# A hybrid decoder layer on one core: the first 256 tokens' trunk rewritten in two halves of 128, with scaling by the root mean square after the first products

## The reference

```python
h = rmsnorm(x, norm_mix)
u_s5, x_lru, y_lru, g_a, g_b = split(h @ w_in)          # 512, 512, 512, 1024, 1024 columns
a_out = S5(u_s5)        # complex diagonal scan over time, 32 groups of 64 states, then gelu, GLU (w_glu)
b_out = RG-LRU(x_lru, y_lru)   # conv of width 4, two gates, real scan over time
merged = sigmoid(g_a) * (a_out @ w_proj_a) + sigmoid(g_b) * (b_out @ w_proj_b)
x = x + merged @ w_out
x = x + peer(rmsnorm(x, norm_ffn))
def peer(xc):           # 8 heads
    q = xc @ w_q;  s = q . sub_keys                     # 2 x 128 scores for each head
    16 best of each 128, 16 best of the 256 sums -> eidx, softmax g
    act = gelu(u_tab[eidx] . xc);  out = sum over 128 experts of g * act * v_tab[eidx]
```

## Time and profile before

| | |
|---|---|
| median of 3 runs | 3243.57 us (3235.98 to 3243.91) |
| profiled execution | 3249.83 us, span 3247.7 us |
| mean granted TensorE clock | 0.934 |
| busy share of the span | PE 84%, PE weight load 48%, DVE 77%, POOL 38%, ACT 30% |
| DMA | 1251.68 MB, mean 385 GB/s; gathers 1082.20 MB |
| first gather issued | 251.13 us |
| largest shares of the chain that ended last | gathers 40%, `values` (L1740) 13%, `dots` (L1410) 10% |

### The profile page before, as it was taken

The page is one execution under the profiler, slowest core; times in us unless marked ns, Lnnn a source line. Parts: engine busy times, 40 slices in busy tenths (PEclk is TensorE's granted clock), DMA queues, the critical chain, the costliest instruction groups (busy, mean ns, idle before and its releaser), DMA issues.

```text
span 3247.7 us, 31396 instructions
## 1 busy us (share of the span) xinstructions
PE 2714.0 (84%) x9120; PEld 1542.8 (48%) x9120; DVE 2493.6 (77%) x5858; ACT 976.4 (30%) x3001; POOL 1225.6 (38%) x1048
## 2 busy tenths in 40 slices
PE   7988988998979989888778989899888895666566
PEld 6874544565445445555334545556434442222122
DVE  6836888888679888887679888887668886666754
ACT  2113433232134332322134332322123432222223
POOL 0003344344343444344343443343344343545553
PEclk9999999999989999999989999998999997878789
DMA  4369999999999999999999999999999999999997
GB/s 136 95 212 396 403 419 420 409 396 419 418 417 385 411 420 419 381 420 419 418 418 400 418 417 403 387 416 374 417 401 418 420 395 298 421 407 421 422 422 332
DMA packets 208636, 1251.68 MB, mean 385 GB/s; under 512 B 27961, under 2 KB 36537, under 8 KB 76369
## 3 DMA queue, kind: packets, MB, share of 16 engines
q0 software_dynamic: 148608, 1082.20, 81.3%
q1 hardware_dynamic: 57344, 158.97, 13.2%
q10 hardware_dynamic: 2512, 8.52, 0.7%
HBM read 1245.05 MB, written 4.55 MB: 385 GB/s over the span
## 4 chain that ended last, share of the span: by engine, by line
DMA 41%; PE 26%; DVE 21%; issue 3%; ACT 3%; DVEq 2%; POOL 2%; ACTq 1%; POOLq 0%
DMA arena<-in_uv,arena 40%; PE psum L1740 13%; DVE arena L1410 10%; PE psum L1661 6%; DVE arena L1015 4%; DVE arena L1007 3%; ACT arena L692 2%; POOL arena L651 2%; PE psum L1784 2%; PE psum L1796 1%; DVE arena L1256 1%; PE psum L1775 1%; PE psum L1674 1%; PE psum L1694 1%; PE psum L1646 1%
## 5 line engine op out<-in xcount | busy, mean ns | idle before, releaser
L1740 PE MATMUL psum<-arena 128*128 128x512 f32 x3192 | 1606.7, 647 | 463.8 <-ACT arena L692 430.8
L651 POOL DMA_INDIRECT arena<-in_uv,arena x1032 | 1221.6, 1184 | 1994.7 <-PE psum L1740 1381.0
L1410 DVE CUSTOM_DVE_ANT_0 arena<-arena 128x1024 f32<-128x1024 f32 x1024 | 1237.2, 1224 | 529.6 <-DMA arena<-in_uv,arena 498.4
L1740 PEld LDWEIGHTS psum<-arena 128*128 128x128 f32 x3192 | 620.2, 202 | 1303.6 <-ACT arena L692 642.1
L692 ACT ACTIVATE arena<-arena 128x128 f32<-128x128 f32 (+3 forms) x2481 | 699.0, 313 | 1633.7 <-DVE arena L1410 1478.4
L1661 PE MATMUL psum<-arena 128*128 128x256 f32 (+1 forms) x2688 | 622.5, 387 | 12.0 <-DVE arena L1015 6.4
L1661 PEld LDWEIGHTS psum<-arena 128*128 128x128 f32 x2688 | 515.4, 193 | 143.5 <-issue 71.3
L1015 DVE SCALAR_TENSOR_TENSOR arena<-arena 128x1024 f32<-128x1024 f32 (+6 forms) x477 | 392.7, 830 | 66.8 <-ACT arena L692 35.9
L1007 DVE TENSOR_TENSOR arena<-arena 128x256 f32<-128x256 f32 (+10 forms) x832 | 285.0, 382 | 24.1 <-issue 1.7
L692 ACT ACTIVATE arena<-psum 128x256 f32<-128x256 f32 (+7 forms) x266 | 107.3, 414 | 554.5 <-PE psum L1661 481.4
L692 ACT ACT_TABLE_LOAD x113 | 145.0, 1283 | 3.9 <-PEq L2040 0.8
(11 more groups left out here) (97 smaller groups left out, 949.4 us busy)
## 6 DMA issues: line engine op xcount, KB each, us to landing
arena<-in_w_in SPq DMA_DIRECT2D x112, 512.0 KB
arena<-in_w_q SPq DMA_DIRECT2D x68, 512.0 KB
arena<-in_w_ab SPq DMA_DIRECT2D x40, 512.0 KB
arena<-in_w_out SPq DMA_DIRECT2D x40, 512.0 KB
arena<-in_uv,arena POOLq DMA_INDIRECT x1032
arena<-in_w_glu SPq DMA_DIRECT2D x16, 256.0 KB
arena<-in_x_tok SPq DMA_DIRECT2D x8, 512.0 KB
arena<-in_keys SPq DMA_DIRECT2D x32, 128.0 KB
```

Source lines behind the costliest of these rows:

```text
L651: pool.indirect_dma_start(uvring[:, r], None, i_["uv"], bass.IndirectOffsetOnAxis(column, 0)).then_inc(uv_in[r], 16)
L1410: V.tensor_tensor_reduce(out=u, in0=u, in1=hn[i // (SLOT // 2)], scale=1.0, scalar=0.0, op0=ALU.mult, op1=ALU.add, accum_out=dots_[:, b % ...
L1740: ins = mm(PV[:, half], dg[:, PAIR * (b % 2) + k], uvring[:, i % UV, at:at + 512], start=(i % (SLOT // 2) == 0), stop=(pe_slots(c, i + 1) ...
```

## The change

Only chunk 0's stretch up to the end of its own steps is rewritten, as one `first_chunk` on each engine; chunks 1 to 3 keep their code, with other counts.

1. **Scaling after the first products.** DVE writes `gb = hT * nmix` as the four parts of `hT` arrive; PE multiplies the four u units with those, the first ahead of the sum of squares, and `scaled_u` multiplies the products with `rstd` on the way out of PSUM (DVE, in place of an ACT copy). `hT` itself is scaled meanwhile, for the units after. SP issues the parameters of the step size first, then `hT`, the first weights, then the rest.
2. **S5 and LRU in halves.** `s5_in_half(k, jp)`, `s5_out_half`, `s5_half`, `lru_half`, `z_half` do the tokens of tile k. Tile 0 goes through S5, LRU, GLU, `mix`, `out` first. Tile 1's S5 stands between `out`, transposes, queries and scores of tile 0 on PE, and around the first list on DVE.
3. **Four heads alone.** Heads 0 to 3 of tile 0 are ranked alone (ALONE = 4), heads 4 to 7 for both tiles, heads 0 to 3 of tile 1 last, two in a round. w_glu is loaded a second time for tile 1, and eight w_q slots in place of four: SLOTS0 = 92.
4. **Steps.** OWN0 = 57 in place of 48, so 71 steps are left for chunk 1's trunk in place of 80. `on_dve` starts at step 57 in chunk 0, not 48. The first steps (t = 96 to 114) run under the lists of heads 1 to 3, `mix` and `out` of tile 1.

The last two pieces of the diff are the heads alone on ACT, and on DVE what follows the norm of tile 0.

```diff
-OWN0 = 48
+OWN0 = 57
+ALONE = 4
-U_MIX0, U_OUT0, U_MIX1, U_Q0, U_OUT1, U_Q1, UNITS0 = 40, 48, (56, 57, 58, 59, 62, 63, 66, 67), (60, 64), 68, 76, 92
+U_GLU1, U_MIX1, U_OUT1, U_Q1, UNITS0 = 64, 68, 76, 84, 100
 SLOTS0 = UNITS0 - 8
+IN_AT, OUT_AT, GATES_AT = (0, 1, 3, 5, 6, 8, 9, 10), (5, 5, 6, 7, 9, 10, 11, 12), 8
-    first, whole, last = (32, 82, 108) if c else (48, 90, 111)
+    first, whole, last = (32, 82, 108) if c else (57, 94, 112)
...
-            weights0 = trunk + mix + out + mix[0:4] + query[0:2] + mix[4:6] + query[2:4] + mix[6:8] + out \
-                + query[4:16] + query[0:4]
+            weights0 = trunk + mix + out + query[0:2 * ALONE] + trunk[28:32] + mix + out \
+                + query[2 * ALONE:] + query[0:2 * ALONE]
...
+            for k in range(KT):
+                if k % 2 == 0:
+                    dve.wait_ge(x0_in[k // 2], 16)
+                ts(gb[:, k, 0:C], hT[:, k, 0:C], nmix[:, k:k + 1]).then_inc(hx_ok, 1)
+            def scaled_u(q):
+                dve.wait_ge(unit, U_U + q + 1)
+                tt(halves(uS[:, q, 0:C]), parities(PB[q % 2][:, 0:C]), parities(rstd[:, 0:C]), ALU.mult).then_inc(ue_ok, 1)
...
+            def s5_in_half(k, jp):
+                q, done = jp // 2, SJ // 2 * k + jp
+                need(pe, bu_read, done)
+                pe.wait_ge(ue_ok, q + 1)
+                for j in (2 * jp, 2 * jp + 1):
+                    o = 32 * (j % 4)
+                    for part in range(2):
+                        for r in range(2):
+                            at, src = 2 * SEG * part + SEG * k, 2 * SEG * r + SEG * k
+                            ins = mm(SB[j % 2][:, at:at + SEG], wT[o:o + 32, QT * (2 * r + part) + q],
+                                     uS[o:o + 32, q, src:src + SEG], start=(r == 0), stop=(r == 1))
+                ins.then_inc(bu_ok, 1)
...
+                for h in range(ALONE):
+                    for s in range(2):
+                        query(U_Q0 + 2 * h + s, s, qT0[:, s])
+                    if h == 2:
+                        soft(0, P, 1, alone)
+                    scores(h, flat(sS0[:, h]), PV[:, h % 2, 0:2 * NKEY])
...
+                pieces(scans[1], PIECES + 1)
+                for _ in single(0):
+                    pass
+                dve.sem_inc(idx_ok, 1)
+                pieces(scans[1], 3 * PIECES)
+                for piece, _ in enumerate(single(1)):
+                    if piece == 0:
+                        a_half(E_GLU1, LATE)
+                    upto(at0_q(1) + piece + 1)
+                    if piece == 1:
+                        mix(0, U_MIX1, LATE, MIXB[0])
+                    if piece >= 1:
+                        mix(piece, U_MIX1 + piece, LATE, MIXB[piece % 2])
```

More of the change, by code:

```diff
@@ L1 @@
+from collections import namedtuple
 from contextlib import ExitStack
@@ L376, in build @@
         hn = [R.take(D) for _ in range(2)]
-        acc = [R.take(D) for _ in range(2)]
+        acc = [R.take(D)]
+        acc1_at = R.at
+        acc.append(R.take(D))
         dg = R.take(2 * PAIR, P)
@@ L1496, in scale, with a_half, single @@
                     stt(hn_at[t], x2_at[t], ss[:, t:t + 1], weights, ALU.mult, ALU.mult).then_inc(hn_ok, 1)
-                early, late = slice(0, P), slice(P, C)
+                def a_half(e, cols):
+                    for q in range(QT):
+                        dve.wait_ge(evac, e + q + 1)
+                        stt(rT[:, q, cols], rT[:, q, cols], 1.0, yS[:, q, cols], ALU.add, ALU.mult).then_inc(a_ok, 1)
+                def single(h):
+                    dve.wait_ge(s_ev, h + 1)
+                    yield from topk(h, P, 1, lambda t: gn[:, h], lambda t: idxn[:, h], sS0[:, h], alone)
@@ L1565, in chunk @@
                         next(gates)
-                    elif not first:
+                    else:
                         conv(c, convs, last)
@@ L1816, in first_lists @@
-                for m in range(3):
-                    mix1(m)
+                    if k == 2:
+                        s5_in_half(1, 1)
+                    elif k == 4:
+                        s5_out_half(1, 0)
+                        s5_in_half(1, 2)
+                    elif k == 6:
+                        s5_out_half(1, 1)
+                        s5_in_half(1, 3)
+                    out(0, 40 + k, k, [(0, P, 0)])
+                s5_out_half(1, 2)
+                s5_in_half(1, 4)
                 pe.wait_ge(hn_ok, 1)
@@ new lines, in first_chunk @@
+                s5_out_half(1, 5)
+                s5_in_half(1, 7)
+                s5_out_half(1, 6)
+                s5_out_half(1, 7)
+                pe.wait_ge(z_ok, 2 * QT)
+                for q in range(QT):
+                    pe.wait_ge(evac, E_GLU1 + q - 1)
+                    apply(U_GLU1 + q, 48 + 2 * ALONE + q, yS, QT, LATE)
+                for m in range(KT):
+                    upto(at1_mix(m))
+                    if m == 0:
+                        pe.wait_ge(lru_ok, 2 * QT)
+                        pe.wait_ge(a_ok, 2 * QT)
+                        pe.wait_ge(bu_read, SJ)
+                    if m >= 2:
+                        pe.wait_ge(mix_ok, KT + m - 1)
+                    mix(0, U_MIX1 - 8 + m, LATE, MIXB[m % 2], rT)
@@ L1876, in chunk @@
                 upto = paced(batches, c)
[L1877 to L1878 removed]
+                steps = s5_steps(c, n)
                 due = [next(steps)]
```

721 lines of the change are left out of this document (456 added, 265 removed).

## The result

The changed kernel takes **3256.57 us** (median of 5 runs, 3252.45 to 3260.43), beside 3243.57 us of the kernel before: ratio 1.0046, 95% interval 1.0030 to 1.0061. It is slower by 0.46%. The forecast, 3239.7 and "no change", was wrong; the range, up to 3258, held the time. (The ratio is that of the record, over all the runs; the two medians alone give 1.0040, 13.0 us.) A second series of the same kernel gave 1.0032 (1.0020 to 1.0044), so its loss is 10 to 15 us. The profiled execution took 3252.45 us, its span 3250.6.

A forecast was written before the change was run, and what follows sets the result against it. Compute was taken to bound the first 251 us, DMA traffic the 3000 us after. Terms: 24.8 - 18 - 1 - 2 = 3.8 us gained, 3246.0 profiled, 3239.7 as median, "no change"; eight in ten 3223 to 3258.

The forecast's parts named there:

- The start: Launch to first gather, where compute sets the pace: first gather at 226.3 us, 24.8 earlier; bounds 219 and 236.
- What the full stretch must carry: From the first gather on: 7.4 MB more left to move at 412 GB/s, 18 us back; total 1254.6 MB.
- First steps, 1 us back: Chunk 0's first steps: ring traffic until about 254 us, gather 8 at 254; 1 us lost, bounds 0 and 8.
- Steps, 2 us back: Nine steps moved from chunk 1's trunk to chunk 0, PE closer to traffic there: 2 us lost, bounds -3 and 10.
- Rival B: First steps, t = 96 to 117, go at the engines' pace: 13 us lost, start slips 5, 3258; chance 0.19.
- A: Start: halves cost half, PE's clock rises early, first gather at 219; 13 gained, 3230, or 3224; chance 0.32.
- C: Start: weights or DVE's table chain hold PE, first gather at 238; 8 lost, 3251; chance 0.09.
- the first gather is early and the traffic behind it is not full: Sign, around and after the first gather, that would show the forecast wrong; expected DMA share 1.0 from 228 us.

The follow-up runs named there:

- e11_more_mb: The kernel before with 3.15 MB of loads that nobody reads added in chunks 1 to 3: ratio 1.0024.
- e1_own57: The kernel before with 57 own steps in chunk 0 in place of 48 and the DVE rows moved with them: ratio 1.0016.
- the mended kernel: The changed kernel with first-steps waits reordered and the very first step ahead of tile 1's GLU and `mix`: 1.0000 with 57 own steps, 0.9993 with 48.
- e10_early52: The mended kernel with 52 own steps in chunk 0: ratio 0.9986, 3240.41 us beside 3244.73 of the kernel before; repeated, 0.9985.
- e5_own48: The changed kernel with 48 own steps in chunk 0 in place of 57, spread over the same 57 units: ratio 1.0023.
- e7_all: The changed kernel with 48 spread own steps, tile 1's columns copied earlier, DVE's first `dots` before its GLU products, and PE's `mix` and step order edited: 1.0010.
- e9_early48: e7_all (48 spread own steps) plus the very first step taken ahead of the second tile's GLU and `mix`: ratio 0.9993.

## Why the prediction was wrong

*The start:* right. 28.5 us against 24.8. The first unit at 11.74 (11.5 forecast), the granted clock 1.00 between 10 and 60 us (2.4 GHz), units' end 60.08 (60.4), `mix` 155.61 (156.9). `s5_in_half` took 1.60 us busy and 1.53 to the next row, near the whole `s5_in`, as chosen (1.9 with its turnround, so 0.3 too much each). The page "TensorE: Matmul & The Clock Gate" of the Trainium skill, section on LDWEIGHTS, had said that a load takes the time of its columns: the trace agrees, 1.46 us for the 16 loads of 32 rows and 128 columns here against 1.52, and 0.73 for the 16 loads of 128 rows and 32 columns in `s5_out_half`. (That is half for a quarter of the columns.) The latter's products fell from 1.53 to 0.89 (1.1 forecast). The first list ended at 222.18, where the exponentials had been allowed until 225.5 and 0.6 more.

*What the full stretch must carry:* right. 33.7 MB by 222 us (33.4 forecast by 226), 1254.65 MB in all (1254.6), 17.3 us for the bytes where 18 stood, and the price per MB by `e11_more_mb`, within its interval.

*First steps, 1 us back:* this is the step that failed; some 10 us were lost from 250 to 520 us. The ninth gather was forecast at 254 and went at 256.14, and the ring's traffic, said to last "until about 254", ended by 250, since the first gather had come earlier too: the overlap that the sum counted on had a hole of 6 us in it, and the share of 250 to 260 fell to 0.69. The early first step alone gave back about 5.5 us. The prediction had even written down the cause, "steps, POOL and PE's `values` all stand behind the GLU", and then priced it at 1. The waits at the second tile's columns, 4.88 and 5.14 us on PE and 14.43 on POOL, had no term at all; moving one copy there gave 5 to 10 by the ratios, 1 to 3 at gather 256.

*Steps, 2 us back:* too small as well; chunk 1's trunk lost about 7 us. `e1_own57` has 5 us for the moved steps alone; in the mended kernel it is 2 (1.0000 against 0.9993, intervals overlapping), or 4.5 to 5 against 52 steps (0.9986 and 0.9985). The working compared PE's sum with the traffic's over the whole trunk, and both fitted; the loss is local, where a chain without steps outlasts the ring (share 0.61 and 0.64 at 990 to 1010 us).

*Rival B* gave 3258, nearly the measured time, and a dip at 250 to 260 us, which came. That its number fits is luck: its mechanism, engines too slow for a step of 6.4 us "below 400 GB/s until 370", is not what happened: from 300 to 350 us the share is 1.02 at 416 GB/s, and changes of order and of the number of steps, which shorten no instruction, took the losses away. Its working also sets 382 GB/s against a 420 that the earlier trace rows doesn't have; against the 412 there its 13 us would be 10. Only its slip of the first steps was real. *A* said 219 for the first gather, as far from the 222.67 measured as the forecast's 226.3; its input halves at half price didn't come, and it failed behind the first gather where the forecast did. *C* didn't come.

The sum, then: 28.5 gained, 17.3 for bytes, 18 lost behind the first gather where 3 stood, about 7 behind at 1200 us. The prediction had named this sign against itself: "the first gather is early and the traffic behind it is not full". The ratios' 10 to 15 us are more than these 7; their intervals reach down to 6.5. Chunks 2 and 3 show no further loss that stands out from single executions: from gather 512 to 640 the changed kernel falls 3.3 us further behind, but there the kernel before took 369.8 us, the least of all the profiles, and the others 370.4 to 374.0. Open too is the rest of the lead: with both losses mended, some 11 us should be left, and `e10_early52` shows 4.5 to 4.9 in its ratios and 5 to 9 at gather 256.

## What to carry to other kernels

Here a transfer that started earlier gained only as many bytes as the buffers held until their first consumer ran: follow the ring's ninth place, not its first, and put the first consumer ahead of any wait that it doesn't need. When work is moved under a trunk or out of it, don't compare sums over the whole stretch; find the longest chain without a step and ask whether the ring outlasts it. Where nearly every byte counts, price added loads at bytes over the measured rate.

## What the runs showed beyond that

- The ring of eight gathers, issued from 222.67 to 231.57 us, was dry by 250: with the weights loaded beside it, the share was 1.01 from 227 to 250 us and 0.46 in the next 2 us. A stretch of 11.5 to 11.8 us without gathers, near 990 us, emptied it too: with 71 steps to 96 units the unused time there was 8.1 us in the changed kernel, with 80 it was 5.2 in the kernel before and 2.0 to 2.6 in `e5_own48`, `e7_all` and `e9_early48`.
- An ACT copy of 1.00 us, one step late, cost a kernel of 3250 us 5 to 10 us by the ratios (1 to 3 at gather 256), through three engines.
- Holding the first gather back by 15 us cost 4 to 8 us (1.0058 against 1.0046 and 1.0032), though the ninth gather didn't move.
